# HGRN products in 32 x 32 blocks instead of 64 x 64, with masks and copies by quarters

## What is computed

```
def step(state, inp):
    qc, lfc, kc, vc = inp
    b = jnp.cumsum(lfc, axis=1)
    diff = b[:, :, None] - b[:, None, :]
    w = jnp.where(causal, jnp.exp(jnp.minimum(diff, 0.0)), 0.0)
    attn = jnp.einsum('bihd,bjhd,bijhd->bhij', qc, kc, w)
    intra = jnp.einsum('bhij,bjhe->bihe', attn, vc)
    cross = jnp.einsum('bihd,bhde->bihe', qc * jnp.exp(b), state)
    new = state * exp(b_last) + jnp.einsum('bjhd,bjhe->bhde', kc * exp(b_last - b), vc)
    return new, intra + cross
```

## Time and profile before

| | |
|---|---|
| median of 3 runs | 3606.19 us (3604.67 to 3606.43) |
| the profiled execution, its own time | 3605.24 us |
| its span in the trace | 3603.1 us |
| PE busy | 3480.9 us (97%) |
| DVE busy | 2816.3 us (78%) |
| ACT busy | 1266.9 us (35%) |
| HGRN stage, layer 1 and layer 2 | about 1430 to 1815 and 3190 to 3585 us |

### The profile page before, as it was taken

One profiled execution on the slowest core, in us unless ns is written; L12 is line 12 of the kernel. 1 busy time (PEld: TensorE's weight loads), 2 busy tenths in 40 slices (PEclk: granted clock), 3 DMA queues, 4 the chain that ended last, 5 costly groups with the idle time before them and its releaser, 6 DMA issues.

```text
span 3603.1 us, 71005 instructions
## 1 busy us (share of the span) xinstructions
PE 3480.9 (97%) x27042; PEld 2525.5 (70%) x27042; DVE 2816.3 (78%) x5663; ACT 1266.9 (35%) x3545; POOL 520.6 (14%) x798
## 2 busy tenths in 40 slices
PE   7999999999999997999999999999999999989998
PEld 6887888888864565555578878887888445555554
DVE  4666678647988998999955766884598799989996
ACT  3422333334431122444453133333344212234443
POOL 0110000100010355000000000001000115620000
PEclk9999999999999997999999999999999999979999
DMA  7443121322234335233432132214323333433332
GB/s 249 153 160 110 61 80 52 113 87 83 77 106 128 118 115 180 90 107 123 138 123 78 72 99 67 74 49 129 95 72 115 95 111 121 143 137 107 106 114 83
DMA packets 248304, 389.39 MB, mean 108 GB/s; under 512 B 30592, under 2 KB 176224, under 8 KB 247840
## 3 DMA queue, kind: packets, MB, share of 16 engines
q1 hardware_dynamic: 178560, 230.04, 20.6%
q0 software_dynamic: 39968, 122.30, 9.0%
q10 hardware_dynamic: 29440, 32.51, 2.9%
HBM read 264.42 MB, written 122.25 MB: 107 GB/s over the span
## 4 chain that ended last, share of the span: by engine, by line
PE 85%; DVE 10%; issue 2%; DMA 1%; ACT 1%; SPq 0%; DVEq 0%; POOL 0%; ACTq 0%; POOLq 0%
PE ps L1257 35%; PE ps L1665 14%; PE ps L1305 9%; PE ps L1448 5%; PE ps L1430 4%; PE ps L1417 3%; PE ps L1421 2%; PE ps L1618 2%; DVE e_t L2410 2%; PE ps L1580 2%; PE ps L1377 1%; PE ps L1483 1%; PE ps L1643 1%; PE ps L1232 1%; PE ps L1317 1%
## 5 line engine op out<-in xcount | busy, mean ns | idle before, releaser
L1257 PE MATMUL ps<-w_sb,s_t 128*128 128x256 f32 x3456 | 825.8, 382 | 7.4 <-DVE s_t L2337 3.7
L1257 PEld LDWEIGHTS ps<-w_sb,s_t 128*128 128x128 f32 x3456 | 628.0, 190 | 95.3 <-issue 13.0
L1257 PE MATMUL ps<-w_sb,hT 128*128 128x256 f32 x2592 | 635.2, 384 | 5.0 <-ACT hT L1816 2.3
L1665 PE MATMUL ps<-wo_sb,mT 128*128 128x512 f32 x1152 | 536.7, 606 | 2.6 <-ACT mT L2069 2.6
L1305 PE MATMUL ps<-w_sb,hT 128*128 128x512 f32 x1152 | 528.0, 601 | 0.5 <-issue 0.5
L1257 PEld LDWEIGHTS ps<-w_sb,hT 128*128 128x128 f32 x2592 | 473.5, 191 | 74.7 <-issue 11.8
L2315 DVE TENSOR_TENSOR row_t<-ps,p_t 128x256 f32<-128x256 f32 x324 | 136.9, 422 | 349.9 <-PE ps L1257 348.5
L1305 PEld LDWEIGHTS ps<-w_sb,hT 128*128 128x128 f32 x1152 | 207.8, 190 | 213.5 <-issue 209.0
L1665 PEld LDWEIGHTS ps<-wo_sb,mT 128*128 128x128 f32 x1152 | 206.8, 191 | 208.1 <-issue 197.8
L1056 POOL DMA_DIRECT2D projected<-row_t x216 | 117.9, 546 | 1441.4 <-DVE row_t L2400 865.6
L1839 ACT ACTIVATE p_t<-ps 128x256 f32<-128x256 f32 x324 | 124.0, 383 | 534.8 <-PE ps L1257 532.4
(11 more groups left out here) (266 smaller groups left out, 5801.9 us busy)
## 6 DMA issues: line engine op xcount, KB each, us to landing
projected<-row_t POOLq DMA_DIRECT2D x288, 256.0 KB, 2.5
w_sb<-in_w_in ACTq DMA_DIRECT2D x40, 512.0 KB, 5.1
hg_raw<-projected SPq DMA_DIRECT2D x72, 256.0 KB, 4.2
out_streams<-y_t POOLq DMA_DIRECT2D x36, 512.0 KB, 4.8
wa<-in_w_ada SPq DMA_DIRECT2D x10, 1536.0 KB, 7.3
hg_braw<-projected SPq DMA_DIRECT2D x108, 128.0 KB, 2.4
hg_raw<-projected SPq DMA_DIRECT2D x36, 384.0 KB, 3.3
mx_t<-mixed SPq DMA_DIRECT2D x36, 384.0 KB, 5.8
```

The source lines that it names most:

```text
L1257: mm = nc.tensor.matmul(ps[:, (u.run + k) % 2, 0:HB], x[:, c], w_blk[:, at[w], c * HB:(c + 1) * HB], start=opens and c == 0, stop=(c == KH ...
L1665: mm = nc.tensor.matmul(ps[:, 6 + g, :], mT[:, t % 2, k, :], wo_sb[:, k, g * GRP:(g + 1) * GRP], start=(k == 0), stop=(k == KC - 1))
```

## The change

Levels 0 to 4 and the diagonal are computed in four blocks ("quarters") of 32 keys and the same 32 queries. Level 5 is computed as 32 keys of a quarter against the 32 queries of the neighbouring quarter (`q ^ 1`), which is just what belongs to it, so it needs no mask any more. Level 6 stays as it was. The matmuls per call are 6 x 4 x 2 = 48 of 32 x 32 for the masked ones, 4 x 2 = 8 for level 5, and 4 of 64 x 64 for level 6: 60 in place of 32. The mask and the sum then run over 6 x 32 columns of two heads (128 x 384 elements) in place of 7 x 64 (128 x 896), and `hg.tc` has 2 x 32 columns. `weights_out` makes ten copies in place of four: two of level 6 (64 partitions), four of level 5 and four of `hg.tc` (32 partitions each). `hg.p_done` is raised once a call in place of twice. A spare tile keeps all addresses behind as they were.

```diff
@@ shape_constants
-    keep = np.zeros((P, SLOTS + 1, 64))
-    j, i = t % 64, np.arange(64)
-    for lv in range(SLOTS):
+    keep = np.zeros((P, SLOTS, QUARTER))
+    j, i = t % QUARTER, np.arange(QUARTER)
+    for lv in range(SLOTS - 1):
...
@@ weights
-                def product(n, keys, queries):
-                    for blk in range(2):
-                        at = slice(blk * 64, (blk + 1) * 64)
-                        to = slice((1 - blk) * 64, (2 - blk) * 64) if n > SLOTS else at
-                        for hp in range(2):
-                            rows_h = slice(hp * HD, (hp + 1) * HD)
-                            last = nc.tensor.matmul(ps[at, 4 + hp, n * 64:(n + 1) * 64], keys[rows_h, at], queries[rows_h, to],
-                                                    start=True, stop=True)
-                            if n > SLOTS and blk == 1:
-                                last.then_inc(hg.p_done, 1)
-
-                for lv in range(SLOTS):
-                    product(lv, hg.k[:, b, lv, g], hg.q[:, b, lv, g])
-                product(SLOTS, hg.xT[:, b, 4 + g], hg.xT[:, b, g])
-                product(SLOTS + 1, hg.k[:, b, LEVELS - 1, g], hg.q[:, b, LEVELS - 1, g])
+                def product(at, to, col, keys, queries):
+                    for hp in range(2):
+                        rows_h = slice(hp * HD, (hp + 1) * HD)
+                        last = nc.tensor.matmul(ps[at, 4 + hp, col:col + to.stop - to.start], keys[rows_h, at], queries[rows_h, to],
+                                                start=True, stop=True)
+                    return last
+
+                quarters = [slice(q * QUARTER, (q + 1) * QUARTER) for q in range(4)]
+                for lv in range(SLOTS - 1):
+                    for at in quarters:
+                        product(at, at, lv * QUARTER, hg.k[:, b, lv, g], hg.q[:, b, lv, g])
+                for at in quarters:
+                    product(at, at, (SLOTS - 1) * QUARTER, hg.xT[:, b, 4 + g], hg.xT[:, b, g])
+                for q, at in enumerate(quarters):
+                    product(at, quarters[q ^ 1], SLOTS * QUARTER, hg.k[:, b, LEVELS - 2, g], hg.q[:, b, LEVELS - 2, g])
+                for blk in range(2):
+                    at, to = slice(blk * 64, (blk + 1) * 64), slice((1 - blk) * 64, (2 - blk) * 64)
+                    last = product(at, to, (SLOTS + 1) * QUARTER, hg.k[:, b, LEVELS - 1, g], hg.q[:, b, LEVELS - 1, g])
+                last.then_inc(hg.p_done, 1)
@@ weights_out
-                    nc.scalar.activation(hg.p[at, :, at], hg.tc[at, :, :], ACT.Copy)
-                    last = nc.scalar.activation(hg.p[at, :, other], ps[at, 4:6, (SLOTS + 1) * 64:(SLOTS + 2) * 64], ACT.Copy)
+                    nc.scalar.activation(hg.p[at, :, other], ps[at, 4:6, (SLOTS + 1) * QUARTER:(SLOTS + 1) * QUARTER + 64], ACT.Copy)
+                for q in range(4):
+                    at, other = slice(q * QUARTER, (q + 1) * QUARTER), slice((q ^ 1) * QUARTER, (q ^ 1) * QUARTER + QUARTER)
+                    nc.scalar.activation(hg.p[at, :, other], ps[at, 4:6, SLOTS * QUARTER:(SLOTS + 1) * QUARTER], ACT.Copy)
+                for q in range(4):
+                    at = slice(q * QUARTER, (q + 1) * QUARTER)
+                    last = nc.scalar.activation(hg.p[at, :, at], hg.tc[at, :, :], ACT.Copy)
                 last.then_inc(hg.p_ready, 2)
@@ masked_hg
-                u, n = l * NT + t, (SLOTS + 1) * 64
-                dve.wait_ge(hg.p_done, HEADS * u + 2 * g + 2)
+                u, n = l * NT + t, SLOTS * QUARTER
+                dve.wait_ge(hg.p_done, 2 * u + g + 1)
```

More of the change, by code:

```diff
@@ L38 @@
 SLOTS = LEVELS - 1
+QUARTER = 32
 KV_AT = 384
@@ L91, in shape_constants @@
         keep[:, lv] = same & ((j[:, None] // s) % 2 != (i[None, :] // s) % 2)
-    keep[:, SLOTS] = j[:, None] == i[None, :]
+    keep[:, SLOTS - 1] = j[:, None] == i[None, :]
     cols["keep"] = keep.reshape(P, -1)
@@ L377 @@
 BLOCKS_AT = 18104
-HG_CORE = 14 * GW + P + 2 * P + 4 * GW + 4 + 12 * P + 16 * P + 8 * LEVELS * P + 8 * P + 128 + (SLOTS + 1) * 64
+HG_CORE = 14 * GW + P + 2 * P + 4 * GW + 4 + 12 * P + 16 * P + 8 * LEVELS * P + 8 * P + 2 * QUARTER + SLOTS * QUARTER
 def count_turns():
@@ L559, in build @@
         hg.qx = sb(s, "hg_qx", [P, 2, 2, 2, P])
-        hg.tc = sb(s, "hg_tc", [P, 2, 64])
-        keep = sb(s, "keep", [P, SLOTS + 1, 64])
+        hg.tc = sb(s, "hg_tc", [P, 2, QUARTER])
+        keep = sb(s, "keep", [P, SLOTS, QUARTER])
         sb(s, "w_sb_first", [P, HT_END + KC * GRP - HG_CORE])
         wo_sb = sb(s, "wo_sb", [P, KC, D_MODEL])
-        hg.w = sb(s, "hg_w", [P, 2, SLOTS + 1, 64])
+        hg.w = sb(s, "hg_w", [P, 2, SLOTS, QUARTER])
+        sb(s, "hg_spare", [P, 2 * (SLOTS + 1) * 64 - 2 * SLOTS * QUARTER])
         hg.p = sb(s, "hg_p", [P, 2, P])
@@ L2049, in take_x @@
                 b, u = t % 2, l * NT + t
-                need(act, hg.p_done, HEADS * (u - 1))
+                need(act, hg.p_done, 2 * (u - 1))
                 need(act, hg.qk_ready, u - 1)
```

## The result

The changed kernel takes **3645.23 us** (median of four runs, 3644.11 to 3649.06) where the kernel before takes 3606.31 us beside it: the ratio is 1.0112, with a 95% interval of 1.0099 to 1.0124. It is slower by 39 us. The forecast was 3616.4 us with a range of 3601 to 3656. Sign and range hold. The loss is nearly four times the one forecast, so terms of the sum were mis-sized. The profiled execution spans 3642.0 us, 38.9 more than before.

A forecast was written before the change was run, and what follows sets the result against it. The prediction took PE to bound the HGRN stage, with DVE's saving worth 0. Bursts +9.4 us and the end of layer 1 +0.8 gave +10.2, moving the median from 3606.2 to 3616.4 us, range 3601 to 3656.

The forecast's parts named there:

- rival A: PE's burst: small records cost 14.5 ns like large ones, burst 1.97 us, 3670 us (3630 to 3670 if partly queued); chance 0.2.
- PE sets the pace, DVE's saving is worth 0: HGRN stage: PE is busy all 21.5 us of a tile and hides DVE's saving of 3.0 us a tile.
- The mask (0.56 for 0.54) and the sum (0.82 for 0.7): DVE, 384 elements in place of 896: mask 0.54 us, sum 0.7 us, together 1.5 us less a call.
- The burst: PE's products of one call: from 1.09 to 1.22 us, +0.13, times 72 bursts +9.4 us.
- the 0.87 us for the weights and the 112 small records: Within PE's burst: 0.04 us for the first weights plus 0.83 for 112 records of 32 columns.
- the change of shape: Inside PE's burst, from 32 x 32 to 64 x 64 blocks before level 6: 0.09 us.
- The copies: ACT's ten copies a call: 1.9 us, +0.84, just covered before PE loads `hg.p`, so 0 in the sum.
- the 0.13 us for 64 elements from PSUM: ACT's small copies out of PSUM: 0.13 us each, from 0.84 ns an element between 256 and 512 elements.
- rival B: ACT becomes the wait: ten copies take 2.9 us, PE waits 0.7 us in 32 tiles, about 3638 us; chance 0.07.
- The edges: Stage starts: shorter mask and sum against longer copies, net about 0, within 0.8 us either way in each layer.
- The end of layer 1: ACT runs without a pause there and PE waits, so the longer copies show in full: +0.8 us, once.
- Rival C: PE's burst: eight blocks run at once without the 7 ns limit, burst 0.71 us, 3580 us; chance 0.09.

The follow-up runs named there:

- e4_short_sum: The kernel before with mask and sum over three of seven slots, the other slots' products computed but not added: 3601.79 us, ratio 0.9986.
- e2_products_only: The kernel before with only the products changed: levels 0 to 5 and the diagonal in 32 x 32 blocks: 3626.93 us, ratio 1.0059.
- e3_copies_only: The kernel before with only ACT's copies changed, ten a call in place of four: 3647.76 us, ratio 1.0119.
- e10_copies_short_sum: e3_copies_only with mask and sum over three of the seven slots, the other slots' products not added: 3632.52 us in one run.
- e6_levels_twice: The changed kernel with the products of levels 0 to 4 issued twice, 100 matmuls a burst in place of 60: 3827.1 us in one run.

## Why the prediction was right, and where its sizes were off

The sign came from the right mechanism: PE sets the pace, its burst gets longer, and what DVE saves counts for nothing. That the time also lies in the range is in part luck. The forecast of 3612.8 to 3621 us, which had half the chance, was missed by 24 us. The upper part of the range, up to 3656, stood there for small blocks at up to 14.5 ns a record. What filled it was a wait that the forecast had put at nothing, and a burst of 1.36 us, far from the 1.97 of rival A.

- **PE sets the pace, DVE's saving is worth 0.** Right. The mask (0.56 for 0.54) and the sum (0.82 for 0.7) came close, and DVE's busy time in a tile was 18.1 for 17.7. e4_short_sum and e2_products_only show it from both sides. The prediction said that the first group's copies end earlier through it, and so counted no wait for them; e3_copies_only and e10_copies_short_sum show this cover at work, worth 0.5 us a tile.
- **The burst: +0.13 forecast, +0.27 measured.** This is 10 of the 29 us missing (0.14 x 72), less 1.7 for the four bursts at half the clock, which got shorter (from 7.7 us together to 7.0). The term that failed is the 0.87 us for the weights and the 112 small records: they took 0.96. I had chosen between 7 ns a record, "read from this very line", and 7.9. Neither was a law: 7 ns is the distance of followers on four tiles of 64 x 64, on eight tiles records started 4.5 ns apart, and what lasts is the supply at 8.35. The rest, +0.05, lies in the last eight records: the change of shape took 0.12, and from the first group of four to the next were 0.107 us where I had used 0.058, a steady distance for blocks that had none ahead of them. (The 0.05 us for the first weights lies, in the kernel before, ahead of the fifth record, which starts 87 ns after the fourth in place of 38, and not in the first record; its size was right.)
- **The pauses for instructions: 0 forecast, 3.5 us measured.** Rival A named "the instructions may not arrive faster" as a way to a long burst. That was the right mechanism, for the steady pace and for the pauses, with the wrong price: it put a record at 14.5 ns.
- **The copies: 1.9 us forecast, 2.5 measured.** The wait behind them is another 12 of the missing us. The failing step is the 0.13 us for 64 elements from PSUM, a straight line drawn through 256 and 512 elements and carried down to 64. The copies of 32 x 64 came 0.225 us apart from PSUM and 0.265 from SBUF; those of 64 x 128 came 0.28 apart where the line said 0.18. At this size an instruction costs nearly its fixed part: of 64 partitions x 128 elements from `hg.tc` it took 0.30 us, of a quarter of the data 0.25. With 2.5 us the point of 2.2 us from which rival B decides is passed, and its wait came, 0.38 us a tile. The forecast had called it covered by 0.27 us of slack and given the rival 0.07. A cover that thin needed a price from a row of that size.
- **The edges.** The start of the stages: 0 within 0.8 for each forecast; the first period of each stage grew by 0.9 us in layer 1 and 0.1 in layer 2 over what every tile grew by, so 1 us. The end of layer 1: +0.8 forecast, +1.45 measured, by the same mis-sized copies.
- **Rival C** had its premise right: eight blocks do run together (the first 32 records). It fell with the supply of instructions.
- **The sum.** 10 us forecast; 12 more in the bursts, 3.5 of them pauses, 12 in the wait, 0.7 at the end of layer 1 and 4 without a known cause make the 39. Both large errors go the same way: a part was cut into smaller pieces, and a piece was priced too much by its share of the data and too little by the instruction.

The Trainium skill (Perfetto Trace Analysis, Optimizing Scalar/DVE Operations) says that every ScalarE operation carries a fixed overhead for access to its data, about 93 ns on SBUF and 51 ns on PSUM, and shows about twice that as latency. Twice those figures and 64 elements at the 0.84 ns of the earlier trace rows make 240 and 156 ns, an estimate by that page. The two groups of small copies took 254 ns from SBUF, near it, and 215 ns from PSUM, well above it. A fixed part in every copy is what argued for rival B.

## What to carry to other kernels

Before you cut blocks to save wasted elements, count instructions on the engine that sets the pace: here 28 matmuls more a burst cost 0.27 us although the array had room, and a saving of 94 us on an engine that was not the bound brought nothing. Price a small operation by a row of that size; where none exists, take the distance between the smallest operations of that engine as the price of a smaller one. Where a cover is thinner than the uncertainty of what it covers, the rival deserves more than a few hundredths.

## What the runs showed of the hardware that I had not expected

- Matmul records on eight tiles of 64 x 32 started 4.5 ns apart at first, then 8.35 ns apart for as long as the small blocks lasted (to record 180 in e6_levels_twice), with a weight load for each: one instruction in 4.2 ns. That pace was the same at a granted clock of 0.5, where the records of the 64 x 64 blocks went from 14.6 to 26.7 ns.
- PE can run out of instructions: 2.2 to 2.9 us passed from the start of an instruction packet until it went on, in all 107 pauses, and dense bursts of 256 instructions cost 12.3 us that way where slower ones of as many cost 0.4.
- Long pauses cost twice: in e6_levels_twice 16 stretches at a granted clock of 0.5 began within 1.6 us of the end of a pause of 2.1 to 4.9 us.
- Streaming 32 queries in place of 64 against 64 keys left the burst at 1.09 us.
- From 64 x 32 blocks to 64 x 64 blocks 0.12 us passed between two starts.
